# A hybrid decoder layer with 32 experts: weight loads of four units from the fifth expert on

## The chip, the cores and the metric

The kernel runs on one core of a Trainium2 chip. The metric is the device time of one execution in microseconds; the time before is the median of three runs, 1040.64 us (1040.07 to 1040.75). One further execution was recorded with the hardware profiler; all rows below come from it.

## The reference

The input is 256 tokens of 1024 float32 values. A first block (RMS norm, one input projection, forgetting attention with 8 heads beside a causal convolution of width 31, one output projection) adds to the residual. Then comes a mixture of experts, which holds nearly all of the weights:

```python
logits = (x @ w_router + b_router)                  # 256 x 32
top_vals, top_idx = lax.top_k(logits, 4)
top_w = jax.nn.softmax(top_vals, axis=-1)           # gates of 4 experts per token
# for each of the 32 experts:
h = x @ w_gu[e] + b_gu[e]                           # 1024 -> 2048
hg = jnp.minimum(h[:, :1024], 7.0); hu = jnp.clip(h[:, 1024:], -7.0, 7.0)
act = (hu + 1.0) * (hg * jax.nn.sigmoid(1.702 * hg))
acc = acc + gate[:, None] * (act @ w_down[e] + b_down[e])   # 1024 -> 1024
```

A last RMS norm closes the layer. Each expert has 12 MiB of float32 weights (8 in `w_gu`, 4 in `w_down`), and all 32 are read once: 402.7 MB.

## The kernel before

**Experts.** The kernel gathers the tokens of each expert (at most 64 go through the main pass) by a matmul with a selection matrix. `up` multiplies them with the expert's `w_gu`, VectorE and ScalarE clamp and gate, PE transposes the result, and `down` multiplies it with `w_down`; a further matmul scatters the result into the residual in PSUM. PE works through the experts strictly in order, and the order of its instructions is written out by hand.

**Units and the ring.** The weights of an expert are cut into 12 units of 1 MiB (128 partitions x 8 KB): 8 units of `w_gu` and 4 of `w_down` (`UNITS`, line 81). `SEQUENCE` (lines 88 to 91) numbers the units of all experts in the order in which PE uses them; only the last two experts are interleaved. The units pass through a ring of 22 places in SBUF (`RING`, line 82). A few of the first units go to spare places instead. After each unit PE adds one to the semaphore `units_used` (lines 1585 and 1613).

**Loads.** `load_sizes` (line 120) cuts the sequence into loads of 1 to 4 units. The first 18 sizes stand in a list; after them a short stretch has single units (`SINGLES`), then loads have two units up to unit `FINE_UP_TO`, and from there on four (`UP_GROUP`, `DOWN_GROUP`), until `FINE_FROM`, the start of the last two experts, where they have two and one again. A load that runs over the end of the ring is issued as two DMAs (`pieces`, line 139).

**Who waits for what.** SyncE (SP) walks through the loads in order. Ahead of each it waits until PE has used up the unit that stands in the last place which the load will fill, and then issues the DMA:

```python
if first >= LAP_END:
    sp.wait_ge(units_used, used_for(first + size - 1))
...
load(k)
```

In the steady laps `used_for(n)` is `n - 21`. All DMAs of a load add to one of 18 semaphores in turn (`load_full`), and PE waits on that semaphore ahead of the load's first unit, for all of the load (`arrived_unit`, line 1551). Between the second expert and the end SP issues nothing but these loads. ScalarE issues one other DMA in the stretch of the change, `b_down` (line 745, 128 KB).

Of the kernel before, what the change touches and what calls it, by code (L numbers as in the profile page):

```python
# [51 lines left out]
def hybrid_layer(nc, x, norm_mix_g, w_in, b_f, b_glu, w_dw, b_dw, ln_g, ln_b, w_out, norm_ffn_g,  # L52
# [7 lines left out]
    E = w_router.shape[1]  # L60
# [20 lines left out]
    UNITS = UP_UNITS + DOWN_UNITS  # L81
# [13 lines left out]
    FIRST_LAP = [n for n in range(RING + len(SPARES)) if n not in SPARES]  # L95
    LAP_END = RING + len(SPARES)
    GAIN_PLACE = UNITS * E + UNITS
    SINGLES, FINE_UP_TO, FINE_FROM = (UNITS * 2 + 8, UNITS * 3 + 2), UNITS * 8, UNITS * (E - 2)

    def ups_used(e):  # L100
        return PLACE[e, UP_UNITS - 1] + 1
# [1639 lines left out]
```

## Time and profile before

| what | value |
|---|---|
| median of three runs | 1040.64 us |
| the profiled execution's own time | 1041.71 us |
| its span, first to last instruction | 1040.0 us |
| PE busy | 1004.2 us (97%) |
| VectorE, ScalarE, GpSimd busy | 243.1, 163.7, 16.5 us |
| DMA over the span | 421.62 MB, mean 405 GB/s |
| mean granted TensorE clock | 0.996 |

The profile gives busy time per engine, the span in 40 slices, the chain of waits that ended last, and for each line its DMA issues with the time until the data had landed. "Landing" is the moment at which the last of the 16 DMA engines that share a transfer reports. Times inside the execution count from the span's start.

### The profile page before, as it was taken

The numbers are of one execution on the slowest core, as the hardware profiler recorded it, in microseconds if no ns is written. First come the engines' busy times: TensorE is split into PE (matmuls) and PEld (weight loads), VectorE is DVE, ScalarE is ACT, GpSimd is POOL, SyncE is SP. The second block draws the span as 40 slices with busy tenths as digits, with TensorE's granted clock in tenths as the row PEclk, the third lists the DMA queues.
The fourth block names the chain that finished last, engine by engine and source line by source line (L and its number), as shares of the span: only waits on it lengthen the run. The fifth ranks groups of instructions, "written<-read, shape, count | busy, mean of one in ns | idle before, by whom it ended". The sixth has DMA issues, their size and how long they took to land.

```text
span 1040.0 us, 10977 instructions
## 1 busy us (share of the span) xinstructions
PE 1004.2 (97%) x4811; PEld 397.6 (38%) x4812; DVE 243.1 (23%) x534; ACT 163.7 (16%) x308; POOL 16.5 (2%) x29
## 2 busy tenths in 40 slices
PE   9999999999999999999999999999999999999996
PEld 7875544333333333333333333333333333333332
DVE  3995341211011111111111112110111112110122
ACT  5144321111011111111111101110111101110112
POOL 4000000000000000000000000000000000000001
PEclk9999999999999999999999999999999999999999
DMA  9995699999999999999999999999999999999994
GB/s 309 392 418 199 222 391 404 413 417 426 427 427 435 427 431 432 429 427 436 423 434 427 435 428 435 429 430 431 430 430 433 426 431 433 427 435 426 423 425 165
DMA packets 33403, 421.62 MB, mean 405 GB/s; under 512 B 4061, under 2 KB 8457, under 8 KB 14410
## 3 DMA queue, kind: packets, MB, share of 16 engines
q1 hardware_dynamic: 31786, 420.57, 96.2%
q8 instruction: 39, 0.64, 0.2%
q10 hardware_dynamic: 1568, 0.33, 0.2%
q14 instruction: 10, 0.08, 0.0%
HBM read 419.82 MB, written 1.05 MB: 405 GB/s over the span
## 4 chain that ended last, share of the span: by engine, by line
PE 73%; DMA 25%; DVE 1%; issue 1%; POOL 0%; POOLq 0%; ACT 0%; SPq 0%; DVEq 0%
PE work L1215 62%; DMA ring<-in_w_gu 25%; PE resid L1215 7%; PE work L1524 1%; PE work L1590 1%; PE work L1548 0%; PE work L1335 0%; PE work L1244 0%; PE work L1434 0%; POOLq L154 0%; DVE main L962 0%; POOL main L559 0%; DVE main L942 0%; DVE main L1128 0%; DVE main L1194 0%
## 5 line engine op out<-in xcount | busy, mean ns | idle before, releaser
L1215 PE MATMUL work<-ring,main 128*64 128x512 f32 (+1 forms) x3080 | 684.8, 595 | 24.1 <-DMA ring<-in_w_gu 22.6
L1215 PEld LDWEIGHTS work<-ring,main 128*64 128x64 f32 (+1 forms) x3080 | 218.4, 138 | 467.9 <-issue 410.4
L1115 DVE TENSOR_SCALAR main<-work 128x512 f32<-128x512 f32 x32 | 22.1, 691 | 566.9 <-PE work L1215 566.9
L749 ACT ACTIVATE main<-main 128x512 f32<-128x512 f32 x32 | 20.2, 630 | 450.1 <-DVE main L1115 450.1
L1215 PE MATMUL work<-ring 128*128 128x256 f32 (+2 forms) x308 | 71.8, 403 | 0.9 <-issue 0.8
L1215 PE MATMUL resid<-main 128*128 128x512 f32 x128 | 67.9, 617 | 0.9 <-DVE main L1186 0.9
L1215 PEld LDWEIGHTS work<-ring 128*128 128x128 f32 (+1 forms) x308 | 55.6, 186 | 15.7 <-issue 8.7
L1215 PE MATMUL work<-bgu_rows,ident 128*64 128x512 f32 (+1 forms) x260 | 60.9, 587 | 0.0
L767 ACT ACTIVATE main<-work 64x512 f32<-64x512 f32 x63 | 37.2, 591 | 134.1 <-PE work L1215 133.4
L1108 DVE TENSOR_SCALAR lent<-count,place,gates 128x64 f32<-128x64 f32 x64 | 17.0, 309 | 144.6 <-PE work L1548 136.8
L908 DVE SCALAR_TENSOR_TENSOR main<-ring,main 128x256 f32<-128x256 f32 x116 | 46.6, 477 | 1.3 <-ACT main L624 1.1
L1215 PE MATMUL work<-main,select 128*64 128x512 bf16 x360 | 44.0, 379 | 0.0
L1122 DVE SCALAR_TENSOR_TENSOR main<-main 128x512 f32<-128x512 f32 x32 | 34.1, 1066 | 1.1
L1215 PEld LDWEIGHTS work<-main,select 128*64 128x64 bf16 x360 | 21.2, 110 | 29.7 <-issue 17.9
L754 ACT ACTIVATE main<-work 128x512 f32<-128x512 f32 x32 | 19.1, 597 | 72.4 <-PE work L1590 72.4
L1215 PEld LDWEIGHTS resid<-main 128*128 128x128 f32 x128 | 19.5, 189 | 27.2 <-issue 27.2
L1215 PE MATMUL resid<-ring,main 128*128 128x512 f32 (+1 forms) x68 | 28.8, 571 | 0.0
L1215 PEld LDWEIGHTS work<-bgu_rows,ident 128*64 128x64 f32 x260 | 18.4, 137 | 22.9 <-issue 9.1
L764 ACT ACTIVATE main<-work 128x256 f32<-128x256 f32 x16 | 6.1, 383 | 131.6 <-PE work L1548 131.6
L1128 DVE TENSOR_TENSOR main<-work,cols 128x512 f32<-128x512 f32 x30 | 20.7, 691 | 13.8 <-PE work L1524 13.8
L1119 DVE TENSOR_TENSOR main<-main 128x512 f32<-128x512 f32 x32 | 22.2, 692 | 5.4 <-ACT main L749 5.4
L1524 PEld LDWEIGHTS work<-ident,lent 128*128 128x128 f32 x120 | 12.6, 140 | 24.3 <-issue 24.3
(202 smaller groups left out, 334.9 us busy)
## 6 DMA issues: line engine op xcount, KB each, us to landing
ring<-in_w_gu SPq DMA_DIRECT2D x36, 4096.0 KB, 42.1
ring<-in_w_gu SPq DMA_DIRECT2D x36, 2048.0 KB, 16.2
ring<-in_w_down SPq DMA_DIRECT2D x18, 4096.0 KB, 42.4
ring<-in_w_gu SPq DMA_DIRECT2D x8, 3072.0 KB, 37.5
ring<-in_w_down SPq DMA_DIRECT2D x11, 2048.0 KB, 15.6
ring<-in_w_down SPq DMA_DIRECT2D x20, 1024.0 KB, 14.1
ring<-in_w_gu SPq DMA_DIRECT2D x15, 1024.0 KB, 24.2
ring<-in_w_down SPq DMA_DIRECT2D x4, 3072.0 KB, 38.4
```

The lines of the kernel that those rows point to most:

```text
L749: nc.scalar.activation(sig_h, gate_h, ACT.Sigmoid, scale=SWIGLU_ALPHA).then_inc(sig_ready, 1)
L754: nc.scalar.activation(to, work[:, act_bank(n), :], ACT.Copy).then_inc(act_t_ready, 1)
L767: return nc.scalar.activation(y_sb[buffer][h][parity * CAP:(parity + 1) * CAP, :], work[h * CAP:(h + 1) * CAP, bank, :], ACT.Copy)
L908: V.scalar_tensor_tensor(acc, u_pad[:, c, j:j + SEQ], dw_cols[:, c, j:j + 1], acc, ALU.mult, ALU.add)\
L1108: done = V.tensor_scalar(weighted[:, t, parity * CAP:(parity + 1) * CAP], count[:, bass.ds(r * CAP, CAP)], place[:, t, bass.ds(e, 1)], gat ...
L1115: V.tensor_scalar(gate_h, work[:, GATE_BANK, :], SWIGLU_LIMIT, None, ALU.min).then_inc(gate_clamped, 1)
L1119: V.tensor_tensor(sig_h, sig_h, gate_h, ALU.mult).then_inc(glu_ready, 1)
L1122: V.scalar_tensor_tensor(gate_h.rearrange("p (b j) -> p j b", b=4), up_h.rearrange("p (j b) -> p j b", b=4), 1.0, sig_h.rearrange("p (j b) ...
L1128: V.tensor_tensor(tok_t.rearrange("p (h b) c -> p b h c", b=4), work[:, OUT_BANK, :].rearrange("p (b h c) -> p b h c", b=4, h=2), cols[:, ...
L1215: return nc.tensor.matmul(out_, lhsT, rhs, start=start, stop=stop, skip_group_check=True)
L1524: last = nc.tensor.transpose(work[:, OUT_BANK, b * P:(b + 1) * P], tok_rows[:, b // 2, b % 2 * P:(b % 2 + 1) * P], ident[:, :])
L1590: last = nc.tensor.transpose(work[:, act_bank(n), j * P:(j + 1) * P], gate_h[:, j * P:(j + 1) * P], ident[:, :])
```

## The change

`FINE_UP_TO` goes from the first unit of the ninth expert (unit 96) to the first unit of the fifth (unit 48):

```diff
-    SINGLES, FINE_UP_TO, FINE_FROM = (UNITS * 2 + 8, UNITS * 3 + 2), UNITS * 8, UNITS * (E - 2)
+    SINGLES, FINE_UP_TO, FINE_FROM = (UNITS * 2 + 8, UNITS * 3 + 2), UNITS * 4, UNITS * (E - 2)
```

Units 48 to 95 are loaded in 12 loads of four units instead of 24 loads of two. Both ways two of these loads run over the end of the ring (68 to 69, and 90 to 91, before; 68 to 71, and 88 to 91, after) and have two DMAs, so there are 14 DMAs instead of 26. The place, the size and the order of all other loads stay; the number of each later load falls by 12, and with it the semaphore that it uses.

## Rows read from the trace of the kernel before

**Rows 1.** The page, the span in 40 slices: DMA share in tenths, GB/s.
```profile
DMA  9995699999999999999999999999999999999994
GB/s 309 392 418 199 222 391 404 413 417 426 427 427 435 427 431 432 429 427 436 423 434 427 435 428 435 429 430 431 430 430 433 426 431 433 427 435 426 423 425 165
```

**Rows 2.** Stretches: busy us of each engine, granted clock, DMA share, GB/s.
```profile
200.00:320.00 120.00, 119.53 (x566) 42.27 (x564) 22.46 (x45) 14.99 (x26) 0.00 (x0) 1.00 1.01 426
320.00:600.00 280.00, 280.00 (x1330) 97.52 (x1328) 45.55 (x90) 33.16 (x57) 0.00 (x0) 1.00 1.00 430
600.00:960.00 360.00, 337.40 (x1578) 115.67 (x1576) 54.66 (x108) 38.38 (x66) 0.00 (x0) 0.99 1.00 430
```

**Rows 3.** The chain that ended last, from 593 us: start, length, what.
```profile
593.29 20.33 PE work L1215 x100
...
619.12 42.31 DMA ring<-in_w_gu
...
896.48 10.10 PE work L1215 x52
...
912.46 43.34 DMA ring<-in_w_gu
955.84 11.80 PE work L1215 x52
...
1017.95 10.47 PE work L1215 x48
```

**Rows 4.** Waits: SP in 150 to 320, PE in 600 to 967 and from 956.
```profile
SPq L435 <- PE work L1215: 148.8, 36, 11.8
...
PE work L1215 <- DMA ring<-in_w_gu: 22.6, 12, 2.5
...
PE work L1215 <- DMA ring<-in_w_gu: 2.1, 1, 2.1
```

**Rows 5.** Line 435, loads issued in 266.5 to 286, then 812 to 854.
```profile
L435 SPq DMA_DIRECT2D ring<-in_w_gu x4: 328/328/328, 266.9 to 285.3; - x4
...
DMA to landing us min/median/max: 12.8/15.2/18.9
...
L435 SPq DMA_DIRECT2D ring<-in_w_gu x4: 327/328/328, 812.2 to 853.7; - x4
...
DMA to landing us min/median/max: 42.7/44.8/45.4
```

**Rows 6.** Line 435, the load issued at 86.1 us.
```profile
L435 SPq DMA_DIRECT2D ring<-in_w_gu x1: 328/328/328, 86.1 to 86.1; - x1
...
DMA to landing us min/median/max: 7.3/7.3/7.3
```

**Rows 7.** Line 435, issues at 189, 196, 208, 216 and 302 us.
```profile
L435 SPq DMA_DIRECT2D ring<-in_w_down x2: 328/537/746, 189.4 to 189.8; - x2
...
DMA to landing us min/median/max: 7.3/8.3/9.4
...
L435 SPq DMA_DIRECT2D ring<-in_w_gu x1: 327/327/327, 196.3 to 196.3; - x1
...
L435 SPq DMA_DIRECT2D ring<-in_w_gu x1: 328/328/328, 208.2 to 208.2; - x1
...
L435 SPq DMA_DIRECT2D ring<-in_w_down x1: 328/328/328, 216.3 to 216.3; - x1
...
L435 SPq DMA_DIRECT2D ring<-in_w_down x1: 328/328/328, 302.4 to 302.4; - x1
...
DMA to landing us min/median/max: 16.5/16.5/16.5
```

**Rows 8.** DMA in 207 to 211 us, while b_down is loaded.
```profile
DMA packets 138, 1.38 MB, mean 344 GB/s; under 512 B 30, under 2 KB 30, under 8 KB 62
```

**Rows 9.** Stretch behind the last wait for weights, columns as in rows 2.
```profile
955.84:959.60 3.76, 3.76 (x10) 1.18 (x12) 0.00 (x0) 0.00 (x0) 0.00 (x0) 0.55 0.97 418
```

## The prediction

> **What bounds the kernel now.** I read the 40 slices first. From the seventh slice to the last but one the DMA engines are busy for nine tenths or more and move 404 to 436 GB/s [rows 1], although PE is shown as busy 97% of the span. So two engines look full, and the question is which of them sets the end. The stretches and the chain of waits answer it together. From 320 to 600 us PE is busy for all of its 280 us; from 600 to 960 it is busy for 337.4 of 360, with the DMA share at 1.00 in both [rows 2]. The 22.6 us that are missing are 12 waits for weights [rows 4]. The chain runs through PE until 593.29 + 20.33 us, and from 619 us on it goes back through one weight load after another, until the load that ends at 955.84 us [rows 3]. The reader should see a ring that starts full and is slowly drained: PE uses weights a little faster than they come, lives on its stock until about 615 us, and from there each expert waits for its loads. PE's last wait for weights ends at 955.84; behind it PE runs to the end without another one [rows 3, 4].
>
> It follows that the stream of loads sets the end although nobody waits for the loads that the change touches. The stream is a queue without gaps from here to 955 us, so a microsecond lost or won at 250 us is handed from load to load and comes out at the last wait, one for one. I therefore cost the change on the DMA stream alone, between two landings: that of unit 47 (issued at 189.8, landed 9.4 later, at 199.2) and that of unit 95 (302.4 + 16.5 = 318.9) [rows 7]. The stretch lasts 119.7 us.
>
> **What the change removes: the cost of a load boundary.** Six two-unit loads that stand in a full queue land from 266.9 + 12.8 = 279.7 to 285.3 + 18.9 = 304.2, five spacings of 4.90 us [rows 5]. Five four-unit loads land from 812.2 + 45.4 = 857.6 to 853.7 + 42.7 = 896.4, four spacings of 9.70 us [rows 5]. Two loads of two need 9.80 us, one of four 9.70: a boundary costs 0.10 us. There are 12 boundaries fewer, which gives -1.2 us. By the rounding of the rows it is between 0.06 and 0.14 per boundary, so -0.7 to -1.7 us.
>
> The Trainium skill, in "DMA: Bandwidth & Descriptors", section "Anatomy of one DMA", gives each DMA a fixed cost of about 2.0 us beside its bytes, mostly the completion's round trip (it is fitted there for another issuing path). By that rule alone 12 DMAs fewer would save some 24 us, an estimate from the page. The spacing of 4.90 us in the queue disagrees where loads queue, since the fixed part lies beside the transfer ahead; what it leaves is the rival below.
>
> **What it adds: a later issue.** A load of four waits for the release of its fourth unit, which is the release that the second of the two old loads waited for, 3 to 12 us after the first. PE is not short of weights here, so these releases don't move: the new loads go out at 196.3, 208.2, 216.3, then 223.1, 235.0, 244.5, 251.4, 266.9, 275.0, 281.9, 293.8 and 302.4 (the first three and the last in [rows 7], the eighth in [rows 5]; the others are read in the same view). That costs nothing as long as the queue ahead of the new load is long enough. How long is enough, the load at 86.1 us shows: it came to an empty queue and landed 7.3 us later, 2.4 us more than the 4.90 of the queued one [rows 5, 6]. A load issued less than 2.4 us before the landing ahead of it therefore leaves a gap of the difference.
>
> With landings 9.72 us apart (I take the upper side of 9.70, and 0.1 more for the two that are split), the margins come out as follows. First load: issued 196.3, the one ahead lands at 199.2, margin 2.9, no gap; it lands at 208.9. Second: issued 208.2, margin only 0.7, gap 1.7; it lands at 220.3. Third: 216.3, margin 4.0, no gap. The next four have 5 to 8 us. The eighth, issued at 266.9 while its predecessor lands at 268.9, has 2.0 and leaves a gap of 0.4. The last four have 4 to 7. Together the gaps are 2.1 us. Below, they could be nothing, if the queue is fed as well as now. Above, the margins are counted to the last of 16 engines, and those that finish earlier stand idle for longer; if a restart cost twice the 2.4 us, the gaps at the first, second and eighth load would be 1.9, 2.2 and about 0.4, some 4.5 us.
>
> **What lies in the gap anyway.** From 207 to 211 us the core moves only 344 GB/s [rows 8], where 430 is the rule [rows 2]: b_down passes through, and the stream loses 4 x (1 - 344/430) = 0.8 us. That is just where the large gap falls, so I take this loss as hidden in it (0 to 0.8).
>
> **The rest of the edit.** SP issues 12 DMAs fewer, at 0.33 us each [rows 5], some 4 us; it waited for PE 148.8 us in 150 to 320 [rows 4], so this is worth nothing. PE waits once per four units instead of twice, and a first unit arrives later by half a load. The ring holds 22 units and PE needs none of these before its stock is used up at about 615 us [rows 3], so that is hidden; were the stock not there, each load would cost PE up to 4.9 us. Behind unit 96 loads have the same sizes, wait for the same releases, and their queue grows (landings 43 to 45 us after the issue late in the kernel, 13 to 19 here [rows 5]), so nothing there restores or adds a gap.
>
> **The sum.** -1.2 + 2.1 - 0.8 = +0.1 us on the stream, carried to the end: the profiled time goes from 1041.71 to about 1041.8 and its span from 1040.0 to 1040.1. The median of the runs is 1.07 below the profiled execution, and I add the change to the median: 1040.7 us.
>
> One term that the change does not control: behind the last wait the granted clock is 0.55 for 3.8 us [rows 9], that is mostly the lower of its two levels, 1.2 GHz, after PE stood for 2.1 us; the 52 matmuls take 11.80 us instead of 10.10 [rows 3]. No later wait absorbs these 1.7 us. A run without the drop is that much shorter, and a slightly shifted stream may have or miss it. It belongs into the range, both ways.
>
> **Rivals.** (a) No gap opens. If the DMA queues start a load that arrives 0.7 us ahead without any idle time, only the boundaries count: 1040.64 - 1.2 = 1039.4 us. For it: in the trace of now the queue never looked empty in this stretch (share 1.01 [rows 2]). Against it: the isolated load's 2.4 us.
> (b) Slower: the queue runs dry at the second load for longer. This is the one place where the margin is under a microsecond. If a restart of four-unit loads takes 4.8 us instead of 2.4, the gaps are the 4.5 us above, and with -1.2 the time is about 1043.9. It decides the verdict as soon as the gaps exceed 3.3 us, since 3.3 - 1.2 is the 0.2% (2.1 us) that a measurement of this kernel can tell from no change. Against it: the release times are PE's and stay, and the margin at the next load is 4.0 us again.
> (c) The saving or loss is taken back before the end, because PE's stock hides it, and the time stays at 1040.6. For it: nobody waits for these loads. Against it: the 12 waits with the DMA share at 1.00.
> (d) Each load pays its start alone, the skill's fixed cost as a mechanism here: 12 loads fewer would save 12 x 2.4 = 29 us of stream, of which PE can use no more than its 22.6 us of waits: 1018 us. Queued loads 4.90 us apart speak clearly against it [rows 5].
>
> **How the numbers follow.** Forecast (about +0.1, from -0.8 to +1.2): 0.55. Rival (a) 0.18, (c) 0.12, (b) 0.08, (d) 0.01; the remaining 0.06 is the clock's 1.7 us or something unseen, half each way. Only (b), (d) and that remainder leave the band of 0.2%: faster 0.05, slower 0.10, within 0.85. The range reaches from rival (a) with a little of the clock's drop below it, 1038.9, to half way to (b), 1042.6.
>
> **What would show it.** In the changed profile the issues of line 435 should stand at 196.3, 208.2, 216.3 and so on; the load issued at 208.2 should land about 12 us later, at 220.3, and the one issued at 302.4 at about 319.0 instead of 318.9. DMA should dip near 209 us and be 430 GB/s elsewhere. PE's last wait for weights should still end within a microsecond of 955.8. I am wrong if the landing at unit 95 moves by over 2 us, if that move does not reappear at 955 us, or if PE waits for weights before 600 us.

## The result, and the profile after

The changed kernel takes 1042.67 us in the median (1040.66 to 1045.19, 17 runs), the kernel before 1040.75 (1039.75 to 1042.91, 17 runs). The ratio is 1.0018 (95% interval 1.0011 to 1.0024), that is +1.9 us (1.1 to 2.5). The forecast was +0.1, and 1042.67 lies just above the range. Two things changed: the median, and the spread between the fastest and the slowest run, which went from 3.2 to 4.5 us.

First two short stretches of the changed kernel and behind them its three long ones, with the columns of [rows 2].

```profile
208.75:210.75 2.00, 2.00 (x11) 0.70 (x12) 0.00 (x0) 0.00 (x0) 0.00 (x0) 1.00 0.91 279
267.50:270.50 3.00, 3.00 (x12) 0.78 (x10) 0.00 (x0) 0.00 (x0) 0.00 (x0) 1.00 0.63 186
200.00:320.00 120.00, 119.53 (x558) 42.64 (x556) 22.22 (x45) 15.01 (x26) 0.00 (x0) 0.99 0.98 418
320.00:600.00 280.00, 280.00 (x1330) 97.32 (x1328) 45.64 (x90) 33.21 (x57) 0.00 (x0) 1.00 1.00 430
600.00:960.00 360.00, 338.32 (x1582) 115.54 (x1580) 54.73 (x108) 38.44 (x66) 0.00 (x0) 0.99 1.00 430
```

The stream is untouched from 320 us on: 430 GB/s, as in [rows 2]. All of the loss lies in 200 to 320, where 426 GB/s have become 418: over 120 us that is 0.96 MB, or 2.2 us at 430. The two short stretches show where it went. Near 209 and near 269 us the queue ran dry. The second place is the emptier one. The kernel before, at these two places (at the first, `b_down` passes in both kernels) and in a stretch that is needed below:

```profile
208.75:210.75 2.00, 2.00 (x10) 0.63 (x10) 0.00 (x0) 0.00 (x0) 0.00 (x0) 1.00 0.93 342
267.50:270.50 3.00, 3.00 (x15) 0.93 (x16) 0.00 (x0) 0.00 (x0) 0.00 (x0) 1.00 1.00 426
261.00:264.40 3.40, 3.40 (x17) 1.61 (x18) 1.47 (x5) 0.60 (x1) 0.00 (x0) 1.00 1.00 424
```

Next the issues of line 435 in the changed kernel that answer to [rows 7] and to the first of [rows 5]: the DMAs ahead of unit 48, then the loads at units 52, 76 and 92.

```profile
L435 SPq DMA_DIRECT2D ring<-in_w_down x2: 328/794/1260, 189.2 to 189.6; - x2
...
DMA to landing us min/median/max: 7.1/8.2/9.2
...
L435 SPq DMA_DIRECT2D ring<-in_w_gu x1: 328/328/328, 208.0 to 208.0; - x1
...
DMA to landing us min/median/max: 13.5/13.5/13.5
...
L435 SPq DMA_DIRECT2D ring<-in_w_gu x1: 328/328/328, 268.3 to 268.3; - x1
...
DMA to landing us min/median/max: 13.9/13.9/13.9
...
L435 SPq DMA_DIRECT2D ring<-in_w_down x1: 327/327/327, 303.8 to 303.8; - x1
...
DMA to landing us min/median/max: 17.4/17.4/17.4
```

Unit 47 lands at 198.8, unit 55 at 221.5, unit 79 at 282.2 and unit 95 at 321.2, where it was 318.9 before. The issue at 208.0 is the forecast one. The one at 268.3 is not: 266.9 was expected. PE had become late, in this stretch of the changed kernel:

```profile
261.00:264.40 3.40, 3.40 (x11) 2.10 (x10) 1.46 (x5) 0.60 (x1) 0.00 (x0) 0.50 1.01 434
```

The granted clock is 0.50 for 3.4 us, the lower of the two levels, 1.2 GHz, and PE gets through 11 matmuls where the kernel before does 17 (its row above). The timeline of PE (start, length, what) shows what it did ahead of that:

```profile
256.52 1.03 PE L1215 MATMUL work<-bgu_rows,ident 128*64 128x512 f32 x4
257.48 3.77 PE L1215 MATMUL resid<-spare,lent 32*128 32x512 f32 x8
261.18 1.11 PE L1524 MATMUL work<-ident,lent 128*128 128x128 f32 x4
262.09 1.06 PE L1590 MATMUL work<-ident,main 128*128 128x128 f32 x4
```

The eight matmuls at 257.48 add the gated `b_down` of all 32 experts, on 32 of the array's 128 rows. They stand in the fifth expert, and behind them the clock fell. The kernel before has the same matmuls; in its profiled execution the clock stayed up.

PE still waits for weights only between 600 and 967 us, 12 times [rows 4]:

```profile
PE work L1215 <- DMA ring<-in_w_gu: 21.7, 12, 2.2
```

and in the chain the last of these waits ends at 958.00 instead of 955.84 [rows 3]:

```profile
915.73 42.23 DMA ring<-in_w_gu
958.00 10.10 PE work L1215 x52
```

The two profiled spans differ by only 0.6 us, because the lower clock behind the last wait [rows 9] is missing in this execution: 10.10 us for the 52 matmuls, not 11.80. One profiled execution of each kernel would have hidden most of the loss.

### The profile page after: what moved, and what is told of

It is laid out like the page before. It is cut to its first block, busy times and chain, and to the rows that moved or that the text cites. A ratio compares the mean times of both kernels' runs of the same rounds, so it can differ in the third digit from the quotient of the medians.

```text
span 1040.6 us, 10965 instructions
## 1 busy us (share of the span) xinstructions
PE 1004.8 (97%) x4811; PEld 396.9 (38%) x4812; DVE 243.3 (23%) x534; ACT 163.9 (16%) x308; POOL 16.5 (2%) x29
## 4 chain that ended last, share of the span: by engine, by line
PE 67%; DMA 25%; DVE 6%; ACT 1%; issue 1%; POOLq 0%; POOL 0%; SPq 0%; DVEq 0%
PE work L1215 56%; DMA ring<-in_w_gu 25%; PE resid L1215 7%; DVE main L908 4%; PE work L1524 1%; PE work L1590 1%; DMA main<-in_x 0%; PE work L1548 0%; PE work L1335 0%; PE work L1244 0%; PE work L1434 0%; DVE main L915 0%; DVE ring L887 0%; DVE ring L918 0%; POOLq L154 0%
```

## The experiments

In the edits, `FINE_UP_TO` is the first unit that is loaded in fours. Each kernel was timed in five rounds beside the kernel before on the same chip. Lateness is a landing against that of the kernel before: the report of the last of the 16 DMA engines or, where the text says so, the mean of their 16 reports.

**Is it the size or the late issue?** Loads of two, issued when the four-unit load would be (all other lines as before):

```diff
-sp.wait_ge(units_used, used_for(first + size - 1))
+sp.wait_ge(units_used, used_for(first // 4 * 4 + 3 if UNITS * 4 <= first < UNITS * 8 else first + size - 1))
```

> Loads of two as before in units 48 to 95, but each waits for the release that the four-unit load of the change waits for, so both halves of a group of four are issued together and late. Theory (the late issue is the whole loss): the gaps near 208 and 269 us appear as in the changed kernel, and the 12 boundaries of 0.1 us are paid as well: +2.5 to +3.3 on before (1043.2 to 1044.0). Rival (the size of the DMAs is the cost, not their issue time): no change, within 0.3 us of before.

Ratio 1.0021 (1.0011 to 1.0031), +2.2 us. The DMAs have the old size and the loss is there, so it is the issue time. That is a little under my +2.5 to +3.3, and the interval (1.1 to 3.2) reaches into it. In its profile the clock fell at the `b_down` matmuls for longer; the issue for unit 76 came at 270.4 and the lateness at unit 95 was 4.4.

**Which gap?** Four-unit loads for units 48 to 55 alone:

```diff
-            elif n < FINE_UP_TO:
+            elif n < FINE_UP_TO and not UNITS * 4 <= n < UNITS * 4 + 8:
```

> Four-unit loads for units 48 to 55 alone, two-unit ones again from 56 to 95. Theory (one gap near 208 us carries the loss): unit 55 lands near 221.5 as in the changed kernel, 1.5 later than before, everything behind it stays late, and the time is +1.3 to +2.0 on before (1042.0 to 1042.8). Rival 1 (four-unit loads cost by themselves): two twelfths of the loss, +0.3. Rival 2 (the loss is the second gap near 269 us, which the four-unit wait at unit 76 opens): about 0, slightly below before.

Ratio 1.0011 (1.0002 to 1.0020), +1.1 us. This is under my +1.3 to +2.0 and above both rivals. Unit 55 lands at 221.6, and by the mean of the 16 engines the stream is 1.2 us late from there to its last unit. The first gap alone costs about 1 us, more than nothing and less than the whole. This kernel keeps ten of the twelve boundaries, 0.7 us at the price measured below; without them some +0.4 would be left, an estimate.

The changed kernel with units 76 to 79 in twos (`elif n < FINE_UP_TO or 76 <= n < 80`):

> The changed kernel with units 76 to 79 in two loads of two, so that the second gap, near 269 us, cannot open (its first half is issued at 254.8). Theory A (only the first gap is a steady loss; the second one was wide in the profiled run because a clock drop at 261 us delayed a release by 1.6 us): +1.3 to +1.9 on before, 0 to 0.6 below the changed kernel. Theory B (both gaps are in every run and share the loss): +0.2 to +1.0 on before.

Ratio 1.0009 (1.0000 to 1.0018), +0.9 us, at the upper end of theory B's band; the interval (0.0 to 1.9) covers that of theory A too. A late release is not quite out of the way here: in its profile the clock fell at 261.2 us, the next four-unit load, at unit 80, went out at 276.8 (274.8 in the changed kernel's second profile below, which has no drop), and the mean lateness grew by 0.6 us there.

**Without the first gap.** Four-unit loads from unit 60 (`FINE_UP_TO = UNITS * 5`), timed in two jobs:

> Loads of four from the sixth expert on (unit 60) instead of the fifth: 9 boundaries fewer than before, and the first four-unit load is issued with some 6.7 us of queue ahead of it. Theory (the loss is the gap that a late issue tears into the load queue near 208 us): that gap is gone; the load issued at 266.9 has a margin near 2.7, so no gap or a small one. The stream is 0 to 0.8 us ahead of before at unit 95 and the time is 1040.0 to 1041.0. Rival (four-unit loads are themselves the cost here, wherever they start): nine twelfths of the measured +1.9, about 1042.2.

Ratio 1.0029 (1.0019 to 1.0039), +3.0 us: my expectation failed, and the rival's number is nearer. The profile has no gap near 208 us and no clock drop near 261 us, but the load at unit 76, issued at 267.1, found 2.0 us of queue and lands at 280.7, just where the changed kernel's second profile below has it, although here no first gap had cost anything. Where the queue runs dry, the release alone sets the time, and a lead won before it is lost. Four-unit loads from unit 60, with units 76 to 79 in twos:

> Four-unit loads from unit 60 on, but two loads of two for units 76 to 79: 8 boundaries fewer than before and neither of the two places where the queue ran dry (unit 52 near 208 us, unit 76 near 269 us). Theory (the loss is the two late issues, and a dry queue restarts at the release, whatever stood before): no gap, and the time is 0 to 0.8 us below before. Rival (something else about four-unit loads in these experts made the start at unit 60 slow, +3.0 in its runs): more than +1.0.

Ratio 1.0008 (0.9999 to 1.0017), +0.8 us; neither side's number. In its profile the clock fell at 261.7 us, and the next four-unit load, at unit 80, was the one that came late.

**Moving the matmuls.** The `b_down` matmuls in the seventh expert instead of the fifth, in the changed kernel:

```diff
-        BDOWN_EXPERT = 4
+        BDOWN_EXPERT = 6
```

> The changed kernel with the eight matmuls that add the gated b_down (3.7 us of PE between the releases of units 55 and 57) moved from the fifth to the seventh expert. Theory: these matmuls and the clock drop that follows them in three of the profiles make the release for unit 76 late; without them it comes near 263.3 and leaves a margin of about 5 to 7 us, so the second gap is gone and the first stays: +0.4 to +1.2 on before. Rival (the second gap carries nothing): as the changed kernel, +1.9, or more.

Ratio 1.0003 (0.9994 to 1.0012), +0.3 us (-0.6 to +1.2), just under my band and clear of the rival's +1.9. The first gap is still there (unit 55 lands at 221.4), but the load for unit 76 goes out at 262.5 and the queue keeps moving:

```profile
L435 SPq DMA_DIRECT2D ring<-in_w_gu x1: 328/328/328, 262.5 to 262.5; - x1
...
DMA to landing us min/median/max: 18.1/18.1/18.1
```

The same move alone, and with the start at unit 60:

> Control: the kernel before, with the b_down matmuls moved to the seventh expert and nothing else. Theory: its two-unit loads have 8 to 15 us of queue ahead of them where these matmuls stand, so a late release there costs nothing and the move gains nothing: within 0.5 us of before. Rival (the move is a gain by itself, about 1 us, and hid a loss in the changed kernel with the same move): 1 us or more below before.

> Four-unit loads from unit 60 on, and the eight matmuls that add b_down moved to the seventh expert, so that no release is late where a four-unit load waits for it. Theory: no gap anywhere, 9 boundaries fewer than before, the stream about 0.8 us ahead at unit 95 and the time 0 to 1.2 below before. Rival (four-unit loads this early cost something besides late issues): +0.8 or more, as the start at unit 60 without the move showed.

The control gives 1.0000 (0.9991 to 1.0009), so the move is no gain by itself. The start at unit 60 gives 0.9997 (0.9988 to 1.0006): with the matmuls out of the way it is 3.3 us better than it was with them in the other job, and level with the kernel before. By the last engine its stream is 0.9 ahead at unit 95, but the control's is 0.8 ahead there too. The mean of the 16 engines tells more: from unit 47 to 95 it gains 0.6 us, which is nine boundaries at 0.07, and the control gains nothing. The timings can't tell that from nothing.

**Clock or PE time?** The same eight matmuls, in the old place, on all 128 rows:

```diff
-mm(resid[...], gates_t[:, t * P:(t + 1) * P], bdown_sb[:, h * HALF:(h + 1) * HALF], False, False)
+mm(resid[...], extra_sel.rearrange("p u h c -> p (u h c)")[:, t * P:(t + 1) * P], spare[:, h * HALF:(h + 1) * HALF], False, False)
```

> Four-unit loads from unit 60 on, with the eight b_down matmuls where they were (fifth expert) but over all 128 rows of the array instead of 32; the 96 further rows hold leftovers, so the output is not the reference's. The time that PE spends there should stay 3.7 us. Theory (the clock drop behind the 32-row matmuls makes the release for unit 76 late): no drop near 261 us, unit 76 goes out near 266.9, and the time is 0 to +1.2 on before, 2 us below the same kernel with 32 rows. Rival (the 3.7 us of PE time alone do it, without the clock): as with 32 rows, +2.0 to +4.0.

> The start at unit 60 with the 32-row matmuls once more, beside the kernel with full rows on one chip: +2.0 to +3.5 on before by the theory, and a profile with a drop near 261 us has unit 79 landing near 282.3, one without near 280.7. Rival (its first time was a chance of that job): under +1.2.

> The changed kernel with the same full-row matmuls (output likewise not the reference's). Theory: no drop near 261 us, only the first gap and a small second one remain: +0.6 to +1.2 on before instead of +1.8. Rival (the drop carries nothing): +1.5 to +2.4.

From unit 60: 1.0011 (1.0003 to 1.0020) with 128 rows and 1.0025 (1.0014 to 1.0037) with 32, on one chip. The changed kernel with 128 rows: 1.0011 (1.0002 to 1.0020), +1.1 us, in the theory's band, though the interval covers the rival's too. Of the two kernels from unit 60, first the stretch behind the matmuls and then the load for unit 76. With 128 rows:

```profile
261.00:264.40 3.40, 3.40 (x18) 1.66 (x18) 1.46 (x5) 0.60 (x1) 0.00 (x0) 1.00 1.01 434
```

```profile
L435 SPq DMA_DIRECT2D ring<-in_w_gu x1: 328/328/328, 267.1 to 267.1; - x1
...
DMA to landing us min/median/max: 14.5/14.5/14.5
```

With 32:

```profile
261.00:264.40 3.40, 3.40 (x13) 1.59 (x14) 1.46 (x5) 0.60 (x1) 0.00 (x0) 0.65 1.01 434
```

```profile
L435 SPq DMA_DIRECT2D ring<-in_w_gu x1: 328/328/328, 268.5 to 268.5; - x1
...
DMA to landing us min/median/max: 13.4/13.4/13.4
```

The matmuls take 3.70 us in both. Without the drop the load leaves 1.4 us earlier. The 32 rows by themselves don't make it late: the first job's profile of the start at unit 60 has them and no drop, and its load left at 267.1 too. The two timings differ by some 1.5 us (1.0025 against 1.0011), but their intervals overlap, and which timed runs had a drop is not on record; that the drop makes this difference is likely and not shown. Nor is it shown that the rows decide on the drop: two profiles with 128 rows have none, but neither have 7 of the 12 with 32 rows in this place. The +1.1 that remains fits the matmuls' own 3.7 us in front of a four-unit wait, which moving them took away as well: with 128 rows and no drop the mean lateness still goes from 0.3 ahead at unit 75 to 1.2 late at unit 79.

**The changed kernel again.**

> The changed kernel once more, for a second profile. Theory (the width of the second gap is set by the clock at the b_down matmuls): if the granted clock drops near 261 us, unit 76 is issued near 268.4 and unit 79 lands near 282; if it doesn't drop, it is issued near 266.9 and unit 79 lands near 280.5, and the stream is then 0.8 to 1.2 us late at unit 95 instead of 2.2. Timed: +1.1 to +2.4 on before, as the first time. Rival (the gap's width has another cause): unit 79 lands near 282 without a drop.

Ratio 1.0017 (1.0006 to 1.0028), the first result once more. This profile has no drop at 261 us, and its issue at 266.7 is the one that I had forecast:

```profile
261.00:264.40 3.40, 3.40 (x19) 1.64 (x20) 1.46 (x5) 0.60 (x1) 0.00 (x0) 1.00 1.01 434
```

```profile
L435 SPq DMA_DIRECT2D ring<-in_w_gu x1: 328/328/328, 266.7 to 266.7; - x1
...
DMA to landing us min/median/max: 14.0/14.0/14.0
```

Unit 79 lands at 280.7, close to the 280.5 that I expected. The lateness at unit 95 missed: 2.3 by the last engine, 0.6 as a mean over the 16. One engine was held up and the others were not. PE waits for all 16, and this profile's span (1040.7 us) is as long as the first one's (1040.6), so in this execution the loss came without a clock drop near 261 us.

**Dose and answer.** The load for unit 76 waits for two more units:

```diff
-sp.wait_ge(units_used, used_for(first + size - 1))
+sp.wait_ge(units_used, used_for(first + size - 1) + (2 if first == 76 else 0))
```

> The changed kernel, with the load at unit 76 waiting for two more units of PE, so that it goes out near 271.6 instead of 266.9. Theory (a dry queue restarts about 2.3 us after the issue, and its lateness is carried one for one to the end): unit 79 lands near 283.6 to 285.5, 3 to 4 us later than with the release of the change, and the time is +4.5 to +6 on before. Rival (the ring's stock of 20 to 30 us absorbs a loss this early, at least in part): less than +3.

Ratio 1.0051 (1.0037 to 1.0064), +5.3 us. Issue 271.6, landing 12.2 later, at 283.8; unit 95 is 5.4 late and the last unit, at the end, 5.0. The ring's stock gives nothing back.

**The price of a boundary, and b_down's transfer.** Loads of two up to unit 191 (`FINE_UP_TO = UNITS * 16`), and the changed kernel with `load_bdown()` behind the fourth expert (`if e == 3`) instead of the third:

> The opposite direction: loads of two up to unit 191 instead of 95, so 24 boundaries more than before and every issue as early or earlier. Theory (a boundary costs 0.085 to 0.10 us of the stream, carried to the end): +2.0 to +2.4 on before. Rival (the boundary cost is hidden, only dry queues count): within 0.3 of before.

> The changed kernel with ScalarE issuing the 128 KB transfer of b_down one expert later, so that it does not run at 207 to 211 us, in the first gap. Theory (the transfer is not hidden in the gap but holds the slower DMA engines past it): unit 55 lands near 220.2 instead of 221.5; the time is 0 to 0.8 us below the changed kernel, since the second gap still follows and is set by its release. Rival (the transfer was hidden): unit 55 lands at 221.5 still.

The first: 1.0016 (1.0007 to 1.0025), +1.7 us for 24 boundaries, 0.07 each (0.03 to 0.11), under my +2.0 to +2.4. Its trace says the same: by the mean of the 16 engines the stream goes from 0.4 ahead at unit 95 to 1.4 late at unit 191, 1.8 us for the 24. The second: unit 55 lands at 208.1 + 13.4 = 221.5 all the same, so the transfer was hidden in the gap and my new theory was wrong there; ratio 1.0010 (1.0001 to 1.0019). Issued at 240.0 instead, outside a gap, the transfer did cost the stream some 0.9 us (mean lateness 0.9 at unit 63, 1.7 at unit 67, where the changed kernel's falls by 0.1).

## Why the prediction was wrong

The frame held. The stream sets the end, a loss at 270 us is there at 955 us one for one (the dose of 4.7 us in the issue shows it best) and the gaps opened at the two loads that the margins named.

*The boundaries* (-1.2): right in kind, and a little large. Their measured price of 0.07 makes it -0.8.

*The first gap* (1.7, less 0.8 for b_down): the restart came as worked out. In the trace of the changed kernel 15 of the 16 engines report unit 55 by 220.1, where I had 220.3; one reports at 221.5, and an instruction fetch of 16 KB runs at 216.0. But I had counted from the last engine, which stood idle least. Over the mean of the 16 reports, the stream loses 1.3 us from unit 47 to 55 (it goes from 0.5 ahead to 0.8 late), where my terms give 0.7 with the two boundaries. The kernel with this gap alone agrees: +1.1.

*The second gap* (0.4): this is the step that failed, in the words "PE is not short of weights here, so these releases don't move". The margin of 2.0 us was read from one execution, and the release that it hangs on stands right behind the 32-row matmuls. In 5 of the 12 profiles that have them in the fifth expert the clock drops near 261 us (not in that of before), and a release comes 1.4 to 3.5 us later. The gap grows with it: by the mean of the 16 engines it costs 1.8 us in the changed kernel's first profile, with the drop (0.5 late at unit 75, 2.3 at unit 79), and 0.4, my number, in the second, without it. With its margins of some 8 us at this place the old kernel doesn't feel this (the control). I had written down the clock's 1.7 us, but only at the end, as noise of both signs; a late release in front of a queue that is nearly dry counts in one direction. The wider spread goes with this gap: the fastest and the slowest run of the changed kernel are 4.5 and 4.7 us apart in its two timings, 2.2 with the first gap alone and 2.1 with the matmuls moved. With 128 rows it is still 4.1, so it is not shown that the drop makes all of it. Even without the drop the matmuls' own 3.7 us are what made the margin small: with them moved the load leaves at 262.5 instead of 266.7.

*The median.* With the second gap gone (matmuls moved) the change costs +0.3, and the +1.1 of the first gap alone, less the 0.7 of the ten boundaries that were kept there, says much the same: +0.4. So some 1.5 of the 1.9 us belong to the second gap, where I had 0.4. With intervals of about 0.9 us to either side the split is rough. Of the rivals, (b), the queue dry for longer, was nearest, but at the wrong load and not by a longer restart: the load at unit 76 that found an empty queue landed 12.2 us after its issue, 9.7 for its data and 2.5 for the restart, and [rows 6] gives 2.4. The Trainium skill ("DMA: Bandwidth & Descriptors", section "Anatomy of one DMA") gives each DMA a fixed cost of about 2.0 us, fitted for another issuing path; the traces here show 2.4 to 2.5, and only where the queue is empty.

*The working itself.* My chain of landings, carried on to unit 95, ends at 317.9 and not at the 319.0 that I named as a sign: the old stretch of 119.7 us holds 2.1 more than 24 spacings of 4.90, and I had set out only the 0.8 of `b_down`. The sum, a difference, doesn't need the rest, but the margins of the later loads do. And half way to rival (b) is 1042.3, not 1042.6.

Still open: how often the clock drops in the timed runs, since only profiled executions show where it does; how much of the loss comes from single engines that are held up, as in the second profile; and why the start at unit 60 was slower (+3.0 and +2.6) than the change itself, when both profiles put its stream no later at unit 95 than that of the change.

## What to carry to other kernels

Where a queue of loads is the bound, a wait for more free buffers costs nothing while the queue ahead is longer than the restart, and then everything, one for one, however much stock lies behind it. Read that margin at each load, for the engine that finishes first, and ask what may make the release late in another execution: one profile gives the margin, not its spread. A tight margin turns noise that was free into a loss of one sign.

## What the runs showed of the hardware

- The granted clock fell to 0.50 for 3.4 us (6.8 in one profile) while the profile shows PE as fully busy, behind eight matmuls on 32 rows: in 5 of 12 profiles with them in the fifth expert, and in 1 of 3 with them in the seventh (at 316.2 us). Behind the same eight on 128 rows it fell in neither of 2, which is too few to tell.
- The 16 engines of one load drift apart over the kernel, by 7 us in the trace of before (the last unit's first report comes at 1017.5 and its last at 1024.5). A dry queue brings most of them together again: in the changed kernel's first profile their reports of unit 47 lie 1.8 us apart, and behind the first gap 15 of 16 report unit 55 within 0.6 us.
